# A two-layer hybrid diffusion backbone: the projection blocks in front of attention in another order, modulation steps spread over more of them

## The reference

```python
sh1, sc1, g1, sh2, sc2, g2 = ada_modulation(c, ada_w[l], ada_b[l])      # silu(c) @ w + b, w is 1024 x 6144
hc, hx = modulate(xc, csh1, csc1), modulate(x, sh1, sc1)
pc, px = hc @ w_in[l], hx @ w_in[l]        # columns: A q 512, k 128, v 128 | B q 256, k 256, v 256 | C 3 x 256
qa = apply_rope(rms_norm(px[A q], q_gain)); ka = apply_rope(rms_norm(px[A k], k_gain))
ox = concat([gqa_latent(qa, ka, va, kca, vca),                     # 8 heads
             neighbourhood_attention(qb, kb, vb, kcb, vcb, rpb),   # 4 heads, q and k not normed
             hyena_mixer(px[C])])
# hyena_mixer(z): z = short_conv(z, 3 taps) + b;  x0, x1, v = split(z);  u = v * x1
#                 y = bidir_long_conv(u, filters) + u * skip;  return y * x0
x = layer_norm(ALPHA * x + g1 * (ox @ w_out[l]))
x = layer_norm(ALPHA * x + g2 * moe(modulate(x, sh2, sc2)))        # 64 experts, 8 of them a token
```

## Time and profile before

| | |
|---|---|
| median of 3 runs | 1529.31 us (1528.6 to 1532.37) |
| the profiled execution | 1529.05 us |
| its span, first to last instruction | 1527.2 us |
| mean granted TensorE clock | 0.928 |
| TensorE matmul busy | 1320.1 us, 86% |
| VectorE, ScalarE, GpSimd busy | 35%, 19%, 20% |

### The profile page before, as it was taken

The page is one execution under the profiler, slowest core; times in us unless marked ns, Lnnn a source line. Parts: engine busy times, 40 slices in busy tenths (PEclk is TensorE's granted clock), DMA queues, the critical chain, the costliest instruction groups (busy, mean ns, idle before and its releaser), DMA issues. The chain is left out here.

```text
span 1527.2 us, 19670 instructions
## 1 busy us (share of the span) xinstructions
PE 1320.1 (86%) x6420; PEld 733.0 (48%) x6421; DVE 538.8 (35%) x1346; ACT 290.7 (19%) x711; POOL 303.7 (20%) x395
## 2 busy tenths in 40 slices
PE   4999997788879999989889689994985799999991
PEld 1443433444445566656556434473543554545440
DVE  5205014456574322213222109245457221111124
ACT  0100001433210122212222211112520011111110
POOL 0000001445203133323232200100610411111000
PEclk9899997899897999999999989997996799999995
DMA  9767669000225899999998296423023799999930
GB/s 339 289 265 283 240 249 309 1 1 1 97 97 187 322 375 376 366 374 373 384 377 331 105 349 257 172 99 101 1 97 124 263 399 387 402 407 400 408 143 28
DMA packets 109724, 373.32 MB, mean 244 GB/s; under 512 B 17946, under 2 KB 24348, under 8 KB 100408
## 3 DMA queue, kind: packets, MB, share of 16 engines
q1 hardware_dynamic: 85752, 313.51, 54.5%
q0 software_dynamic: 23008, 55.40, 9.8%
q10 hardware_dynamic: 864, 3.15, 0.5%
HBM read 368.78 MB, written 30.47 MB: 261 GB/s over the span
## 5 line engine op out<-in xcount | busy, mean ns | idle before, releaser
L1239 PE MATMUL bank<-weights,b_qk 128*64 128x256 f32 (+2 forms) x1040 | 160.2, 384 | 4.4 <-DVE b_qk L2114 2.5
L1239 PEld LDWEIGHTS bank<-weights,b_qk 128*64 128x64 f32 (+2 forms) x1040 | 110.9, 147 | 63.9 <-issue 36.5
L2120 DVE TENSOR_TENSOR expert_act<-silu_a,bank 128x128 f32<-128x128 f32 x76 | 21.9, 288 | 310.7 <-ACT silu_a L1529 310.7
L1271 PE MATMUL bank<-tokens_h,a_k 128*128 128x512 f32 x208 | 103.7, 622 | 0.0
L1261 PE MATMUL bank<-weights,expert_act_T 128*64 128x512 f32 (+2 forms) x260 | 91.8, 617 | 8.6 <-DMA weights<-in_exp_w 4.9
L2308 POOL DMA_INDIRECT shift_scale_gate_norm<-scratch_h,gather_index x82 | 84.8, 1034 | 71.3 <-POOL gather_index L2305 66.6
L1239 PE MATMUL bank<-features_h,b_qk 128*32 128x256 f32 (+2 forms) x512 | 95.2, 381 | 0.4
L1059 PE MATMUL bank<-weights,features_h 128*128 128x512 f32 x192 | 86.2, 604 | 0.8 <-ACT features_h L1342 0.8
L2114 DVE COPY b_qk<-bank 128x512 f32<-128x512 f32 x78 | 53.9, 692 | 80.7 <-PE bank L1227 80.6
L1227 PE MATMUL bank<-tab,shift_scale_gate_norm 128*128 128x128 f32 x624 | 82.2, 275 | 0.0
L1529 ACT ACTIVATE silu_a<-bank 128x128 f32<-128x128 f32 x76 | 21.1, 278 | 315.0 <-PE bank L1239 315.0
(11 more groups left out here) (325 smaller groups left out, 2021.4 us busy)
## 6 DMA issues: line engine op xcount, KB each, us to landing
weights<-in_exp_w SPq DMA_DIRECT2D x195, 512.0 KB, 10.4
shift_scale_gate_norm<-in_ada_w SPq DMA_DIRECT2D x48, 1024.0 KB, 6.7
features_h<-in_exp_w SPq DMA_DIRECT2D x64, 512.0 KB, 9.7
qkv<-in_exp_w SPq DMA_DIRECT2D x64, 512.0 KB, 15.0
a_q<-in_exp_w SPq DMA_DIRECT2D x32, 512.0 KB, 12.4
weights<-in_w_in SPq DMA_DIRECT2D x6, 2048.0 KB
shift_scale_gate_norm<-scratch_mod POOLq DMA_DIRECT2D x16, 512.0 KB, 8.9
probs_T<-in_exp_w SPq DMA_DIRECT2D x16, 512.0 KB, 15.5
```

The source lines that it names most:

```text
L1239: mm = pe.matmul(ab[r, 0:2 * HIDDEN].rearrange("p (m h) -> p m h", m=2), XGT[:, u.slot() % 2, k, r], expert_w13(slot)[:, :, k, :], start=k ...
L1271: mm = pe.matmul(ACC[g][h][:, :], GROW[:, u.slot() % 2, g * P:(g + 1) * P], YSB[:, u.slot() % 2, h * HALF:(h + 1) * HALF], start=False, st ...
L2120: tt(ACTV[:, :], SIL[:, :], ab[:, HIDDEN:2 * HIDDEN], ALU.mult).then_inc(L["act"], 1)
```

## The change

`c` blocks go in front of the `b_qk` blocks. The b_qk blocks are spread: 0 and 1 behind the q and k transposes, 2 behind the u transposes, 3 behind `scores(0)`. The inverse transform and its two closing steps on VectorE come behind block 3, so between the first and second pair's scores. Weight items follow that order (win 0, 1, 3, 4, 2). For that the convolution no longer writes to `OT`: x0 and u lie in the unused half of ring slot `win 4`, x1 and the products' scratch in `probs`; w_out's first half, which follows in that slot, waits for the long convolution. The convolution starts a block as soon as that block is copied. Modulation steps go by fixed counts: 2 behind each q block, 3 behind each kv block, 2, 2, 2, 2, 3, 3 behind the c blocks, 3 and 3 behind b_qk 0 and 1; none stand alone, and the wait for their reading moves to the first `product`. The bias row of the modulation moves to `router_w`'s memory, whose load waits for the last group.

```diff
+ADA_Q, ADA_KV, ADA_C, ADA_BQK = (2, 2, 2, 2), (3, 3, 3, 3), (2, 2, 2, 2, 3, 3), (3, 3, 0, 0)
...
-        items += [("win", l, b) for b in range(5)] + [("mixc", l), ("wo", l, 0), ("wo", l, 1)]
+        items += [("win", l, b) for b in (0, 1, 3, 4, 2)] + [("mixc", l), ("wo", l, 0), ("wo", l, 1)]
...
-        ADAB = QA_[:, 1408:1408 + HALF]
+        ADAB = RW.rearrange("p k e -> p (k e)")
...
+        def gate_and_u(l):
+            return item(("win", l, 4)).rearrange("p (k c) -> p k c", k=KD)[:, :, 256:512]
...
+                if n >= RING and items[n - RING][0] == "win" and items[n - RING][2] == 4:
+                    sp.wait_ge(by_vector, jobs.of[("yh", items[n - RING][1], 1)][2])
...
+                        else:
+                            sp.wait_ge(ada_filled, DEPTH * ADA_GROUPS)
                         load(RW, a["router_w"][l].rearrange("(p k) e -> p k e", k=KD), router_in)
...
+            def ada_steps(many):
+                for _ in range(many):
+                    ada(*divmod(ada_at[0], KD))
+                    ada_at[0] += 1
...
-                w = arrived(("win", l, 2)).rearrange("p (k c) -> p k c", k=KD)
-                for f in range(4):
+                for f in range(6):
+                    w = arrived(("win", l, 3 + f // 4)).rearrange("p (k c) -> p k c", k=KD)
+                    b = start(("c", l, f))
...
+                    if l == 0 and f == 3:
+                        columns(1)
+                    if l == 0:
+                        ada_steps(ADA_C[f])
+
+                def queries_keys(f):
+                    w = arrived(("win", l, 2)).rearrange("p (k c) -> p k c", k=KD)
                     lo = first if f < 2 else 0
                     b = start(("bqk", l, f))
...
                     if l == 0:
-                        ada(3, 2 * f)
-                        ada(3, 2 * f + 1)
+                        ada_steps(ADA_BQK[f])
...
-                if l == 0:
-                    for k in range(KD):
-                        ada(5, k)
-                    pe.wait_ge(ada_read, DEPTH * ADA_GROUPS)
...
+                queries_keys(0)
+                queries_keys(1)
                 pe.wait_ge(u_ready, l + 1)
...
-                        mm = pe.transpose(b[:, ct * P:(ct + 1) * P], OT[:, 2 + ct, t * P:(t + 1) * P], ident)
+                        mm = pe.transpose(b[:, ct * P:(ct + 1) * P], u_rows[:, 4 + 2 * ct + t // 2, (t % 2) * P:(t % 2 + 1) * P], ident)
                     mm.then_inc(bank_filled, 1)
+                queries_keys(2)
...
                     if i < n:
                         scores(i)
+                    if i == 0:
+                        queries_keys(3)
+                        long_conv()
+                        read_out(("bqk", l, 3))
+                    if l == 0 and i == PV_LAG:
+                        pe.wait_ge(ada_read, DEPTH * ADA_GROUPS)
...
                     if i < n:
                         exponent(2 * i + 1)
+                    if i == 0:
+                        queries_keys(3)
...
-                dve.wait_ge(by_scalar, jobs.of[("c", l, 5)][2])
...
+                for f, z in enumerate((*x0, *x1, *us)):
                     def w(i):
                         return HYC[:, l, 3 * f + i:3 * f + i + 1]
-                    z = OT[:, f, lo:HALF].rearrange("p (s t) -> p s t", t=SEQ)
+                    dve.wait_ge(by_scalar, jobs.of[("c", l, f)][2])
...
-                link(tt(OT[:, 2:4, lo:HALF], OT[:, 2:4, lo:HALF], OT[:, 4:6, lo:HALF], ALU.mult))
+                for ct in (0, 1):
+                    link(tt(us[ct], us[ct], x1[ct], ALU.mult))
                 dve.nop().then_inc(u_ready, 1)
...
                         dve.reciprocal(RC[:, U % 4:U % 4 + 1], SM[:, U % 4:U % 4 + 1]).then_inc(sums_inverted, 1)
+                    if i == 0:
+                        long_conv()
```

More of the change, by code:

```diff
@@ L289, in plan @@
             jobs.add(("kT", l, t), "scalar")
+        for f in (0, 1):
+            jobs.add(("bqk", l, f), "scalar")
         for t in full:
             jobs.add(("uT", l, t), "scalar")
+        jobs.add(("bqk", l, 2), "scalar")
         for m in (0, 1):
@@ L929, in _ @@
                     if l == 0:
-                        ada(2, 2 * t)
-                        ada(2, 2 * t + 1)
+                        ada_steps(ADA_KV[t])
                 first = full[0] * P
-                w = arrived(("win", l, 2)).rearrange("p (k c) -> p k c", k=KD)
-                for f in range(4):
+                for f in range(6):
+                    w = arrived(("win", l, 3 + f // 4)).rearrange("p (k c) -> p k c", k=KD)
+                    b = start(("c", l, f))
+                    for k in range(KD):
+                        mm = pe.matmul(b[:, first:HALF], w[:, k, (f % 4) * P:(f % 4 + 1) * P], HT[:, k, first:HALF],
+                                       start=k == 0, stop=k == KD - 1)
+                    mm.then_inc(bank_filled, 1)
+                    if l == 0 and f == 3:
[4 more added lines that the diff above has]
+                    w = arrived(("win", l, 2)).rearrange("p (k c) -> p k c", k=KD)
                     lo = first if f < 2 else 0
@@ L991, in _, with long_conv @@
                         mm.then_inc(bank_filled, 1)
[L992 to L1001, removed]
+                def long_conv():
+                    pe.wait_ge(yf_ready, 2 * (l + 1))
+                    for ct in (0, 1):
+                        b = start(("yh", l, ct))
+                        for s in range(ns):
+                            for m in (0, 1):
+                                for cs in (0, 1):
+                                    mm = pe.matmul(b[:, s * SEQ:(s + 1) * SEQ],
+                                                   YF[:, m, cs, s * C_CH + ct * P:s * C_CH + (ct + 1) * P],
+                                                   inv[:, m, cs, :], start=m + cs == 0, stop=m + cs == 2)
+                        mm.then_inc(bank_filled, 1)
                 for t in range(TILES):
@@ L1408, in _ @@
                     ada(2)
[L1409 to L1414, removed]
                 act.wait_ge(pads_ready, l + 1)
@@ L1420, in _ @@
                                               b[:, first:HALF].rearrange("p (s t) -> p s t", t=SEQ)))
-                    if l == 0 and f == 0:
+                    if l == 0 and f == 1:
+                        ada(3)
+                    if l == 0 and f == 3:
                         columns(1)
-                    if l == 0 and f == 3:
+                    if l == 0 and f == 5:
                         ada(4)
-                if l == 0:
-                    ada(5)
                 for t in range(TILES):
@@ L1432, in _, with queries_keys @@
                     drained(("kT", l, t), copy(KA0[:, t * P:(t + 1) * P], b[:, 0:P]))
+                def queries_keys(f):
+                    b = filled(("bqk", l, f))
+                    lo = first if f < 2 else 0
+                    drained(("bqk", l, f), copy(BQK[:, f, lo:HALF], b[:, lo:HALF], HEAD ** -0.5 if f < 2 else None))
+                queries_keys(0)
+                queries_keys(1)
+                if l == 0:
+                    ada(5)
                 for t in full:
@@ L1830, in _ @@
                     link(stt(z, CP[:, f, s0:2, 2:SEQ + 2], w(2), z, ALU.mult, ALU.add))
[L1831 removed]
+                for ct in (0, 1):
+                    link(tt(us[ct], us[ct], x1[ct], ALU.mult))
                 dve.nop().then_inc(u_ready, 1)
[L1834 removed]
+                T1, T2 = PB[:, 0, 0:ns * C_CH], PB[:, 1, 0:ns * C_CH]
                 T1, T2 = (x.rearrange("p (s c) -> p s c", s=ns) for x in (T1, T2))
```

44 lines of the change are left out of this document (18 added, 26 removed).

## The result

The changed kernel takes 1478.44 us (median of 4 runs, 1476.28 to 1479.73), the kernel before 1530.84 beside it: a ratio of 0.9651, 95% interval 0.9621 to 0.9681. Timed again with 6 runs against another set, it took 1483.83 us, ratio 0.9697 (0.9669 to 0.9726). The median of its ten runs is 1479.5. Forecast: 1481, range 1474 to 1492.

What follows compares the result with a forecast made beforehand. TensorE, busy 86% of the span, was taken to bound the kernel, with recoverable idle and low clock in both layers' mixer fronts. 22.6 + 25.4 = 48.0 us off 1529.05 gave 1481 us, range 1474 to 1492.

Steps and rivals of the forecast that it cites:

- Layer 1, 22.6 us: Layer 1's mixer front up to scores(3): reordered blocks cover the u, inverse transform and first softmax waits, saving 22.6 us.
- Layer 0, 25.4 us: Layer 0's mixer front up to scores(3): covered waits and full clock save 25.4 us, with 3.1 us of wait left.
- Late next: the second softmax: Attention's start in layer 1: second softmax comes late, product(0) waits about 2 us and transposed(1) about 0.5.
- Modulation steps at 0: Layer 0's key/value stretch: weights for the spread steps keep up at 338 GB/s, so waits cost 0.
- the 6 us bound: Upper bound on weight waits in the key/value stretch: at 293 GB/s it takes 46.4 us, 6 more.
- w_out at 0: Later issue of w_out's first half costs 0, landing in 7.4 us; bound 3 us each layer.
- ScalarE's copy: Fourth block's copy between exponents: 0.6 us under TensorE's block, no second table load; otherwise 2.6 us a layer.
- Starved steps: Rival: loads keep only 293 GB/s and a wait per layer is 2 us longer; 1491 us, chance 0.14.
- All covered, clock kept: Rival: residual waits vanish and layer 0's first attention pairs run at full clock; 54 us saved, 1475, chance 0.09.
- One layer giving it back: Rival: w_out or the attention loop absorbs one layer's gain; 1504 to 1507 us, chance 0.06.
- Slower by the ring's pace: Rival: layer 0's modulation weight loads at 231 GB/s take 43 us more; 1524 us, chance 0.03 including other losses.
- The sum: Both layers' mixer fronts together: 22.6 + 25.4 = 48.0 us saved, later stages shifting unchanged.

Runs made afterwards that it cites:

- conv_waits_all: Changed kernel, but VectorE's convolution starts only when all six c blocks are copied; 1489.52 us.
- fourth_early: Changed kernel with the fourth b_qk block moved ahead of the forward transform; stretches 7.2 and 7.4 us longer, no total time given.
- scores1_first: Changed kernel with the second pair's scores ahead of the inverse transform and its maxima ahead of the long convolution's closing steps; 1479.14 us.
- steps_stacked: Changed kernel with modulation steps bunched, twelve behind c block 5 and none behind b_qk blocks; 1499.57 us.
- spread_only: Kernel before with only the modulation steps spread, all blocks in their old order; 1538.04 us, ratio 1.0061.
- kv_four: Changed kernel with 4 modulation steps behind each kv block and fewer behind the c blocks; 1486.88 us.
- layer1_old: Changed kernel with layer 1 put back in the order of the kernel before; 1502.67 us.
- wout_late: Changed kernel with w_out's first half held until the seventh pair's scores; issued 10.6 us later in layer 0, no total time given.

## Why the prediction was right, point by point

- *Layer 1, 22.6 us.* Measured 22.95 (81.28 to 58.33). The 8.96 us u wait went by meeting: 992.14 against 992.26. conv_waits_all shows how level it is. The first softmax and inverse transform waits went because of the fourth block; fourth_early brought part of them back, the waits at the sizes of the walk.
- *Layer 0, 25.4 us.* scores(3) came 25.3 earlier (the table's 26.4 holds also 0.4 us by which the kv blocks began later and 0.7 in the pairs behind). Luck has a part in that: two errors cancel. The wait in front of the first product was 1.5 us, where I had 3.1 in all, and 1.7 us went to low clock behind `columns(1)`, which I had not seen coming.
- *Late next: the second softmax.* The place is right (scores1_first removes it), the size was 1.27 us in layer 1 instead of 2 plus 0.5. (The waits that I name there, 0.2, 2 and 0.5, are 2.7 us; my 22.6 against 24.5 without a wait holds 1.9.)
- *Modulation steps at 0.* No wait for weights in either trace of the changed kernel. The stretch moved 331 GB/s at 0.86 share, where I had 338. The Trainium skill's 341 GB/s ("DMA: Bandwidth & Descriptors", section Bandwidth) is for one transfer of 1 MB, and I used it as the pace of a stream. With four such loads in flight the trace of steps_stacked shows 420 GB/s over eight steps, so it does not bind here. The waits of 1.34 us in spread_only (344 GB/s) and 1.87 in kv_four's kv stretch (375) show that 0 holds by a small margin, and that the 6 us bound was too wide.
- *w_out at 0.* Right, but the first half takes about 11.8 us from issue to its reader in layer 0 (263.56 to 275.38), not 7.4: I had priced 2.1 MB at 282 GB/s, and from 263.5 to 275.3 the core moved 221 (212 in the same stretch of the changed kernel), part of it other loads. Why it moved no more was not tested.
- *ScalarE's copy.* No second table load, as the Trainium skill says of Copy ("ScalarE: Activation LUTs", section Table sets): one load at 1009.86, the copy at 1012.50, the next exponent at 1016.75.
- *Rivals.* Starved steps: fell, the key/value stretch took 40.0 us and not 46.4. All covered, clock kept: the sum of its kind was nearly reached in the first execution's time, but not by its mechanism, since both product waits are there. One layer giving it back: fell by layer1_old. Slower by the ring's pace: fell, the last step of layer 0 ended 124 us after the first kv block began.
- *The sum.* 48.0 against 25.3 + 22.95 = 48.2 at the named points. Counted from the first kv block in layer 0 and from the first b_qk or c block in layer 1, the first pair of traces gives 25.7 and 22.95, the second pair 25.8 and 22.9: this repeats. The medians differ by 52.4 in the first comparison, whose interval (48.8 to 58.0 us) just leaves 48 out; the second gives 41.8 to 50.5. The first trace's remaining 4 us are in unchanged code and did not repeat.

What I had not asked is whether the parts are worth anything alone. They are not additive. In layer 0's stretch spreading alone costs 4.8 us, since the lone steps, waits and all, had covered VectorE's convolution; the new order with the steps bunched (twelve in a row, where the kernel before has eight) saves 8.7; both together save 26.4. So spreading pays once the c blocks stand in front. The new order with exactly the old counts of steps was not run.

## What to carry to other kernels

An engine's wait may be hiding another engine's work. Before removing it, name what becomes late in its place; here the steps could be spread only because the independent blocks were kept back to cover each chain of the other engines (convolution, products, first softmax). Walk the engine's order with durations at full clock and the other engines' chains beside it: that gave 48.0 of 48.2 us here, with two errors of some 1.6 us that cancelled. And read an edit of a few microseconds by a stretch between two named instructions, since whole executions vary by more.

## What the runs showed of the hardware that I had not expected

- A wait on TensorE costs more than its length, and between 2 and 6 us the extra hardly grows with it. The block behind a wait of 2.25 us took 1.70 us longer than at full clock (conv_waits_all), behind 3.31 us 1.67 (fourth_early), behind 4.56 and 5.82 us 1.50 and 1.65 (wout_late); behind the 11.34 us of spread_only it was 2.7 (1.97 us instead of 1.09, then 8.86 instead of 7.03). The 1.52 us wait in front of layer 0's first product was followed by nothing in the first trace of the changed kernel; in the second the next groups took 1.12, 1.12 and 1.23 us instead of 0.66, 0.66 and 0.70, and so or nearly so in conv_waits_all, kv_four and fourth_early.
- The clock also fell without idle time. `columns(1)`, 32 matmuls of 4 columns in 3.55 us that count as busy, was followed by a spell at the lower level in 13 of the 14 traces: the two steps behind it took 2.89 to 3.64 us instead of 1.92 in the changed kernel and all its variants, 2.48 in spread_only (there behind 0.41 us of idle) and 2.50 in the second trace of before, but 1.93 in its first. The Trainium skill ("TensorE: Matmul & The Clock Gate", section Part 1: The HAM clock gate) says that the clock is set by how busy TensorE has been; in these rows the trace shows it busy, and the clock fell all the same.
